# Attention steps placed directly behind the query projection, and another order of the first expert loads

## The reference

```python
u, v, q = proj[..., :256], proj[..., 256:768], proj[..., 768:]
y_pool = pool_mixer(u, w_pool, pool_scale)            # window means 2/4/8/16 minus the token, a linear map
a, gate = split(v); glu = a * sigmoid(gate)
y = depthwise_conv(glu, 31 taps) + b_dw
y_conv = silu(layer_norm(y, conv_norm_g, conv_norm_b))   # mean and variance over 256 channels, per token
y_mem = softmax(q @ k^T / sqrt(128)) @ v_mem          # 4 heads, 256 memory tokens, k and v from mem_n @ w_kv
x = layer_norm(alpha * x + concat(y_pool, y_conv, y_mem) @ w_out)
scores = sigmoid(x @ w_router); top 8 of 64 experts per token
x = layer_norm(alpha * x + routed experts + 1 shared expert)   # each (silu(x@wg) * (x@wu)) @ wd, width 256
```

## Time and profile before

| | |
|---|---|
| median of 3 runs | 1431.15 us (1430.84 to 1432.0) |
| the profiled execution | 1432.97 us, of which 1431.4 us is the span from its first to its last instruction |
| TensorE busy / VectorE busy | 1319.7 us (92%) / 966.2 us (68%) |
| mean granted TensorE clock | 0.959 of full speed |

### The profile page before, as it was taken

How to read it: one execution, slowest core, us unless ns; L and a number is a source line. 1 busy time by engine, 2 the same in 40 slices (tenths; PEclk the granted TensorE clock), 3 DMA queues, 4 the chain that set the end, 5 groups by cost and what they waited for, 6 DMA issues and landing times.

```text
span 1431.4 us, 25695 instructions
## 1 busy us (share of the span) xinstructions
PE 1319.7 (92%) x6367; PEld 1087.3 (76%) x6368; DVE 966.2 (68%) x1120; ACT 799.1 (56%) x1057; POOL 467.3 (33%) x430
## 2 busy tenths in 40 slices
PE   8967936799999699999999999999999999999974
PEld 6865725578887588888888888888888888888851
DVE  4889657467766387757579555556677579777737
ACT  4121256412225396857579566556767578777724
POOL 0000020136655243333344333333333344333322
PEclk9989978799999899999999999999999999999988
DMA  6112041122334999888799978788899899999755
GB/s 238 45 53 80 0 175 40 59 84 80 89 110 157 363 320 329 306 308 278 237 329 372 312 219 257 240 252 301 251 310 316 273 327 347 331 329 322 210 178 228
DMA packets 77969, 324.11 MB, mean 226 GB/s; under 512 B 22560, under 2 KB 24768, under 8 KB 52720
## 3 DMA queue, kind: packets, MB, share of 16 engines
q1 hardware_dynamic: 43056, 251.05, 47.1%
q0 software_dynamic: 33728, 68.47, 20.5%
q10 hardware_dynamic: 1152, 4.19, 0.7%
HBM read 290.51 MB, written 67.72 MB: 250 GB/s over the span
## 4 chain that ended last, share of the span: by engine, by line
PE 80%; DVE 11%; DMA 3%; issue 2%; ACT 1%; POOL 1%; SPq 0%; POOLq 0%; ACTq 0%; DVEq 0%
PE ps L1650 37%; PE ps L1668 18%; PE ps L1443 7%; PE ps L1557 6%; PE ps L1468 4%; DVE cv L1030 4%; PE ps L1593 2%; PE ps L1681 1%; PE ps L1582 1%; PE ps L1544 1%; DVE whl L944 1%; DMA sum_d<-ysb,idx 1%; POOL list_d L548 1%; DVE pr L1125 1%; DMA xin<-in_x 1%
## 5 line engine op out<-in xcount | busy, mean ns | idle before, releaser
L1650 PE MATMUL ps<-wgu,xTe 128*128 x2304 | 550.3, 394 | 2.2 <-issue 2.0
L1650 PEld LDWEIGHTS ps<-wgu,xTe 128*128 128x128 f32 x2304 | 426.8, 188 | 89.9 <-issue 4.4
L601 POOL DMA_INDIRECT sum_d<-ysb,idx x95 | 176.2, 1854 | 510.6 <-ACT ysb L829 439.5
L1668 PE MATMUL ps<-wdn,hT 128*128 (+1 forms) x1236 | 299.4, 391 | 0.0
L1311 DVE TENSOR_TENSOR wgu<-raw,wgu (+1 forms) x128 | 287.7, 2289 | 8.4 <-issue 3.5
L1668 PEld LDWEIGHTS ps<-wdn,hT 128*128 128x128 f32 x1236 | 232.7, 189 | 48.4
L757 ACT CAST wgu<-raw (+1 forms) x128 | 246.9, 1930 | 1.6 <-SPq L424 1.6
L1316 DVE TENSOR_TENSOR xTe<-ps,xTe 128x512 fp32r<-128x512 f32 x194 | 124.6, 685 | 141.3 <-ACT xTe L824 141.3
L829 ACT ACTIVATE ysb<-ps,idx 128x512 f32<-128x512 f32 x188 | 119.3, 686 | 122.5 <-PE ps L1668 122.5
L1311 DVE TENSOR_TENSOR wdn<-raw,wdn x64 | 146.7, 2293 | 59.5 <-ACT wdn L817 59.1
L591 POOL DMA_INDIRECT xg<-x_d,idx x99 | 110.2, 1113 | 49.5 <-issue 27.5
(11 more groups left out here) (226 smaller groups left out, 1152.6 us busy)
## 6 DMA issues: line engine op xcount, KB each, us to landing
raw<-in_w_gate SPq DMA_DIRECT2D x64, 1024.0 KB, 11.4
raw<-in_w_up SPq DMA_DIRECT2D x64, 1024.0 KB, 8.6
raw<-in_w_down SPq DMA_DIRECT2D x64, 1024.0 KB, 9.3
wraw<-in_w_in SPq DMA_DIRECT2D x10, 512.0 KB, 3.4
xin<-in_x SPq DMA_DIRECT2D x8, 512.0 KB, 7.3
wraw<-in_w_kv SPq DMA_DIRECT2D x8, 512.0 KB, 3.2
raw<-in_w_out SPq DMA_DIRECT2D x4, 1024.0 KB, 8.1
xres<-in_x SPq DMA_DIRECT2D x8, 512.0 KB, 5.1
```

What stands on the lines that cost most here:

```text
L601: g.indirect_dma_start(out=sums, out_offset=bass.IndirectOffsetOnAxis(ap=idx[:, c % RING, c % 2:c % 2 + 1], axis=0), in_=ysb[:, c % 2], in ...
L1650: last = mm(ps[:, 2 + s, :], xTe[:, s, st, d], wgu[:, w, mo, d].rearrange("p a n -> p (a n)"), start=(d == 0 and st == 0 and mo == 0), sto ...
L1668: last = mm(ps[:, down_bank(i) + h, :], hT[:, s, st, c], wdn[:, w, mo, c, h * 512:(h + 1) * 512].rearrange("p a n -> p (a n)"), start=(c = ...
```

## The change

In the projections: `memT` is split in u0; u0 and u1 have 8 taps each, q1 4, q2 9 and q3 13; the pooling parts stand in q0 (three) and q1 (two), and `pool0`, `pool1` behind q1. The jobs `mean` and `var` are gone from `JOBS`, as is the meeting of the engines at `s_endP`. The LayerNorm of the convolution is done within the tiles of the attention: mean behind the first two `scores`, its subtraction ahead of tile 0, squares in tile 0, the sum of squares in tile 1 as 16 products with one column each (a variance per token along partitions), its power -0.5 on GpSimd for 8 elements per partition, a diagonal matrix of it on DVE in tile 2 (`spread`), its product with the matrix of 1/256 on PE in tile 3 (constants 2^-16 and -0.5 make up for the 1/256), the scaling on DVE and Silu on ACT in tile 3. PE waits for the scaling before the transposes of tile 3. `w_out` lands in a buffer of its own (`wor`) and is split in tiles 4 to 7.

In the experts: SP loads expert 2 one matrix after the other without waiting for the list, and expert 3 only when the first two gathers have landed. GpSimd reads the number of items and the first three list addresses before it waits for the last scatters.

```diff
@@ jobs @@
-        JOBS = W_JOBS[:15] + ["pool0", "pool1"] + W_JOBS[15:17] + ["mean", "q3", "var"]
+        JOBS = W_JOBS[:16] + ["pool0", "pool1"] + W_JOBS[16:18]
-        TAPS_IN = {"gate1": 8, "a1": 4, "u0": 10, "u1": 10, "q0": 8, "q1": 8, "q2": 6}
+        TAPS_IN = {"gate1": 8, "a1": 4, "u0": 8, "u1": 8, "q1": 4, "q2": 9, "q3": 13}
-            POOL_IN = ["K2", "K3", "V0", "V1", "V2"]
+            POOL_IN = {"q0": (0, 1, 2), "q1": (3, 4)}
@@ SP @@
-                sp.dma_start(raw[:, 2 + n], a["w_out"][n]).then_inc(s_wo[n], 16)
-            sp.wait_ge(s_endP, 4)
+                sp.dma_start(wor[:, 2 * n:2 * n + 2].rearrange("p c n -> p (c n)"), a["w_out"][n]).then_inc(s_wo[n], 16)
+            sp.wait_ge(s_mix, 2)
...
                 load(e, 0, slot_of(e0, 0))
+                if e0 == 2:
+                    landed(e0, 0, rounds)
...
                 load(e, 1, slot_of(e0, 1))
+                if e0 == 2:
+                    landed(e0, 1, rounds)
...
-            sp.wait_ge(s_idx[0], 16)
             load_expert(2, 0)
+            for s in range(2):
+                sp.wait_ge(s_xg[s], 16)
             load_expert(3, 0)
@@ GpSimd @@
-            g.sem_inc(s_endP, 1)
-            g.wait_ge(s_endP, 4)
+            g.wait_ge(s_norm_v, 1)
+            g.tensor_tensor(rv[:, 1], rv[:, 0], half8[:], ALU.pow).then_inc(s_rstd, 1)
+            g.wait_ge(s_mix, 2)
...
+            g.wait_ge(s_tabs, 1)
+            n_items = g.value_load(nit[0:1, 0:1], min_val=NT + E, max_val=MAX_ITEMS)
+            firsts = [g.value_load(tab[0:1, 2, RING + j:RING + j + 1], min_val=0, max_val=LIST - 128)
+                      for j in range(3)]
             for s in range(2):
                 g.wait_ge(s_sc[s], 16 * K * 4)
-            g.wait_ge(s_tabs, 1)
-            n_items = g.value_load(nit[0:1, 0:1], min_val=NT + E, max_val=MAX_ITEMS)
...
             for j in range(3):
-                load_pairs(1, j)
+                g.dma_start(idx[:, j], list_d[bass.ds(firsts[j], 128), :]).then_inc(s_idx[j], 16)
@@ ScalarE, in the attention loop @@
+                if t == 0:
+                    centred_squares()
...
+                if t == 3:
+                    conv_out()
+                if t >= 4:
+                    wo_hi(t - 4)
@@ VectorE @@
+            def centre():
+                v.wait_ge(s_norm_pe, 1)
+                for c in range(2):
+                    step(V.tensor_tensor(cv[:, c], cv[:, c], ps[:, 6:8, :].rearrange("p a n -> p (a n)"), ALU.subtract))
+            def variance():
+                v.wait_ge(s_norm_pe, 2)
+                V.tensor_scalar(rv[:, 0], ps[:, 6, 0:NT], EPS, 2.0 ** -16, ALU.add, ALU.mult).then_inc(s_norm_v, 1)
+            def spread_rstd():
+                v.wait_ge(s_rstd, 1)
+                V.tensor_tensor(spread[:], ident[:].unsqueeze(1).to_broadcast([128, NT, 128]),
+                                rv[:, 1].unsqueeze(2).to_broadcast([128, NT, 128]), ALU.mult).then_inc(s_norm_v, 1)
+            def scale():
+                v.wait_ge(s_norm_pe, 3)
+                for c in range(2):
+                    step(V.tensor_tensor(cv[:, c], cv[:, c], ps[:, 6:8, :].rearrange("p a n -> p (a n)"), ALU.mult))
...
+            centre()
             probabilities(0)
             for t in range(NT):
+                if t == 1:
+                    variance()
+                if t == 3:
+                    scale()
...
+                if t == 2:
+                    spread_rstd()
...
+                if t >= 4:
+                    wo_lo(t - 4)
@@ TensorE @@
+            def conv_variance():
+                pe.wait_ge(s_sq, 1)
+                for t in range(NT):
+                    for c in range(2):
+                        last = mm(ps[:, 6, t:t + 1], buf1[:, c, t * 128:(t + 1) * 128], ones[:, 0:1],
+                                  start=(c == 0), stop=(c == 1))
+            def conv_rows():
+                pe.wait_ge(s_norm_v, 2)
+                for h in range(2):
+                    last = mm(ps[:, 6 + h, :], ones[:], spread[:, 4 * h:4 * h + 4].rearrange("p a n -> p (a n)"),
+                              start=True, stop=True)
...
             scores(0)
             scores(1)
+            conv_mean()
+            pe.wait_ge(s_gfree[0], len(JOBS) // 2)
             for t in range(NT):
                 if t + 2 < NT:
                     scores(t + 2)
+                if t == 1:
+                    conv_variance()
+                if t == 3:
+                    conv_rows()
+                    pe.wait_ge(s_yn, 1)
```

More of the change, by code:

```diff
@@ L109, in build @@
         wrt = at("wrt", 176, [128, 2, ND, E], R)
-        pr = at("pr", 184, [128, 2, HEADS, M])
+        pr = at("pr", 193, [128, 2, HEADS, M])
+        rv = at("rv", 207.125, [128, 2, NT])
+        spread = at("spread", 185, [128, NT, 128])
         oh = at("oh", 194, [128, K, E])
@@ L164, in build @@
         mv = at("mv", 206.90625, [128, 2, 2])
-        sm = at("sm", 192, [128, 2, 3, HEADS])
+        sm = at("sm", 201.75, [128, 2, 3, HEADS])
+        half8 = at("half8", 201.84375, [128, NT])
         tokf = at("tokf", 207.03125, [128, 2])
@@ L212, in build @@
         s_cvd = sem("s_cvd")
+        s_norm_pe = sem("s_norm_pe")
         s_yc = sem("s_yc")
         s_sq = sem("s_sq")
-        s_sd = sem("s_sd")
+        s_norm_v = sem("s_norm_v")
+        s_rstd = sem("s_rstd")
         s_yn = sem("s_yn")
@@ L498, in _ @@
             g.memset(epst[:], EPS).then_inc(s_pool, 1)
-            g.wait_ge(s_pool, 5)
+            g.memset(half8[:], -0.5).then_inc(s_pool, 1)
+            g.wait_ge(s_pool, 6)
             g.affine_select(out=ident[:], in_=ident[:], compare_op=ALU.not_equal, fill=1.0, base=0,
@@ L668, in _ @@
                     nc.scalar.copy(memT[:, 0, 4:8], mtmp[:, 4:8]).then_inc(s_mhi, 1)
-                if w != "mean" and w != "var":
-                    act.wait_ge(s_job, j + 1)
+                act.wait_ge(s_job, j + 1)
                 if w[:4] == "gate":
@@ L690, in _, with centred_squares, conv_out, wo_hi @@
                     nc.scalar.activation(mixA[:, c], both, ACT.Copy, scale=cpar[:, 3, c:c + 1]).then_inc(s_gfree[s], 1)
[L691 to L709, removed]
+            def centred_squares():
+                act.wait_ge(s_yc, 1)
+                nc.scalar.activation(buf1[:, :, 0:S], cv[:], ACT.Square).then_inc(s_sq, 1)
+            def conv_out():
+                act.wait_ge(s_yn, 1)
+                for c in range(2):
+                    nc.scalar.activation(mixA[:, 2 + c], cv[:, c], ACT.Silu, bias=cpar[:, 2, c:c + 1],
+                                         scale=cpar[:, 1, c:c + 1]).then_inc(s_mix, 1)
+            def wo_hi(n):
+                act.wait_ge(s_wo[n], 16)
+                nc.scalar.copy(wo[:, 0, 2 * n:2 * n + 2], wor[:, 2 * n:2 * n + 2]).then_inc(s_wohi, 1)
+            act.wait_ge(s_diff, 1)
+            for n in range(2):
+                act.wait_ge(s_gfree[n], len(JOBS) // 2)
             def q_hi(t):
@@ L1043, in _ @@
                     v.sem_inc(s_mtc, 1)
[L1044 removed]
+                if w == "u0":
                     for b_ in range(2):
@@ L1067, in _ @@
                                         ALU.subtract).then_inc(s_gfree[1], 1)
[L1068 to L1088, removed]
-            assert tap == len(taps)
-            for n in range(4):
+                for part in POOL_IN.get(w, ()):
+                    pooling(part)
+            assert tap == len(taps)
+            settle()
+            v.sem_inc(s_cvd, 1)
+            def centre():
+                v.wait_ge(s_norm_pe, 1)
+                for c in range(2):
+                    step(V.tensor_tensor(cv[:, c], cv[:, c], ps[:, 6:8, :].rearrange("p a n -> p (a n)"), ALU.subtract))
+                settle()
+                v.sem_inc(s_yc, 1)
@@ new lines, in variance @@
+            def variance():
[9 more added lines that the diff above has]
+                    step(V.tensor_tensor(cv[:, c], cv[:, c], ps[:, 6:8, :].rearrange("p a n -> p (a n)"), ALU.mult))
+                settle()
+                v.sem_inc(s_yn, 1)
@@ L1488, in _ @@
                         last = mm(ps[:, b + h, :], bd[:, c], diff[:, c, h * 512:(h + 1) * 512], start=True, stop=True)
-                elif w in ("mean", "var"):
-                    pe.wait_ge(s_const, 8)
-                    pe.wait_ge(s_cvd if w == "mean" else s_sq, 1)
-                    src = cv if w == "mean" else buf1
-                    for h in range(2):
-                        for c in range(2):
-                            last = mm(ps[:, b + h, :], ones[:], src[:, c, h * 512:(h + 1) * 512],
-                                      start=(c == 0), stop=(c == 1))
                 last.then_inc(s_job, 1)
@@ L1501, in _, with conv_mean @@
                         transpose_tile(memin[:, m], 2 * m).then_inc(s_mt, 1)
-            pe.wait_ge(s_job, len(JOBS))
-            pe.sem_inc(s_endP, 1)
-            pe.wait_ge(s_endP, 4)
+            def conv_mean():
+                pe.wait_ge(s_gfree[1], len(JOBS) // 2)
```

(19 more changed lines are left out.)

12 lines of the change are left out of this document (5 added, 7 removed).

## The result

| | before | changed |
|---|---|---|
| median | 1431.58 us (1430.84 to 1433.16, 4 runs) | 1412.08 us (1408.09 to 1413.79, 4 runs) |
| span of the profiled execution | 1431.4 us | 1411.8 us |

The ratio is 0.9853, interval [0.9834, 0.9872]: 19.5 us faster. The forecast was 1403 us, the range 1396 to 1413. The sign and the range held; the number is 9 us too low.

What follows compares the result with a forecast made beforehand. TensorE, busy 92% of the span, was taken as the bound, so only its waits counted: −22 up to the first projection and −6.2 at the first gathers, −28.2 on 1432.97, gave 1404.8, so 1403 us beside the median; range 1396 to 1413.

Steps and rivals of the forecast that it cites:

- the projections: Projections up to the last tap: it ends at about 172 us and the attention starts there instead of 206.92, −35.
- the attention: From the queries' split to the first output projection: 13 us added to 65.9, so that projection starts at 251 instead of 272.86.
- The variance products: In the attention's tile 1: 16 products of one column each, taken as 4.2 us, bounded by 1 and 14.
- the term of −6.2: At the turn to the experts: the first gather lands 5.3 us earlier, and 0.9 us comes from the clock.
- 0 to 2.5 us are added, and I take 1.2: Ahead of the first gathers: expert 2's loads in flight make the last scatters land 1.2 us later.
- three issues: Between the wait for scatters and the gather: three issues at 0.9 us remain, so the gather is issued 2.4 us earlier.
- The term's 0.9 us for the clock: PE's first pieces behind the first gather: a shorter idle may hold the clock, saving 0.9 of 3.3 us.
- My first rival: At the turn to the experts: the first gathers bring nothing, only 0 to 2.4 us are left, 1407 to 1409; chance 0.17.
- its second way: At the last scatters ahead of the first gathers: they land late by as much as the gather would gain.
- its first: At the first gathers: a gather takes its 9 us by itself, even without loads beside it.
- nothing lost behind it: Behind the first gathers, in the expert loop: PE waits nowhere, so the whole −28.2 us reaches the end.
- my rival of a loop bound by transfers: Expert loop of 97 items: 0.29 us per item would undo the gain, at 0.35 us 1437; chance 0.03.

Runs made afterwards that it cites:

- The old order: The changed kernel with taps, `memT` and pooling in the order of the kernel before, LayerNorm still inside the attention: 0.9871 of the kernel before.
- the loads held: The changed kernel with expert 2's three loads also waiting until both first gathers have landed: 0.9805 of the kernel before, 1406.43 us.
- the experts' part alone: The kernel before with only the new order of the first expert loads and of GpSimd's register reads: 0.9982 of the kernel before, 1430.63 us.

## Why the prediction was right in sign and 9 us off

**Right: the projections.** K0's wait is gone, K1's is 4.48 us (4.5 forecast), the last tap ends at 173.4 (172). DVE's wait for the last weight is 5.95 (5.7). The old order shows that the new one is needed for the early split of the queries: without it q3 is late (how much of that reaches the end stays open, as said above).

**Right in this profile: the attention.** From the queries' split to the first projection it takes 77.9 us (251.42 − 173.53), 12.0 more than before (13 forecast), and the first projection stands at 251.4 (251 forecast). The variance products, the one cost without a row, took 4.06 us (4.2). That was in part luck. In six other profiles with the same work ahead of it, the first projection stands between 251.4 and 254.5, and the four at 253.8 or later all have the variance products at 6.82 us, as the changed kernel's first repeat has:

```profile
190.00 6.82 PE L1536 MATMUL ps<-ones,buf 128*128 128x1 f32 x32
```

The granted clock was 0.50 there from 190.5 to 196.5 us, and 0.88 in the first profile from 189.5 to 193.4. The forecast took these products from transposes at the higher level and had no term for the lower.

Silu starts 1.30 us after the start of its table load, and the load starts where the cast ahead of it ends (208.40 + 0.59), so no drain shows. The Trainium skill (page "ScalarE: Activation LUTs", section "What ACT_TABLE_LOAD costs") puts a switch at about 2.66 us with its drain; this case's trace disagrees with it.

**Wrong: the first gathers, the term of −6.2.** Of its parts, the gather's own time was right (4.54 us, 3 to 5 forecast). The step that failed is "0 to 2.5 us are added, and I take 1.2" for what expert 2's loads do to the last scatters, together with the list pieces, which were given three issues and no price for a load in flight. In the changed kernel GpSimd came through the wait for the scatters 3.8 us later than before, counted from the first projection (191.9 against 188.1; 191.4 and 191.7 in the repeats). The list piece took 3.5 us (4.5 and 4.0 in the repeats, 2.0 to 2.2 with no load in flight). The first ate 2.6 us more than the forecast had, the second about 2; the gather itself was 0.5 us shorter than the sum had it. The term's 0.9 us for the clock didn't come either: the first product took 7.09 us, against 7.15 before; with the loads held it took 6.25. The writes of the shared expert's results were slowed as well (ACT waits of 5.2, 4.0 and 3.8 us for them in the three profiles of the changed kernel), which stood nowhere in the sum, but PE waits for the gather behind them anyway.

With no load in flight the stage is 6.2, 6.0 and 5.3 us shorter than before in the three profiles where the gather is waited for and the reads stand ahead. That the first of these equals the forecast's sum is chance: the forecast had loads in flight, 5.3 us up to this point and 0.9 behind it. My first rival, that the gathers bring nothing, is what happened, by its second way (late scatters and what follows them), not by its first: a gather does take half the time when it has the DMA engines to itself. The rival's own time, 1407 to 1409, was too low by what was lost elsewhere.

The Trainium skill, page "DMA: Bandwidth & Descriptors", section "Queues, rings and completion order", has the DMA engines take turns between queues packet by packet. I drew from this that a gather never waits for SP's backlog. The rows don't contradict the rule but do contradict what I drew from it: taking turns with 4 MB doubled the gather (8.93 and 9.24 against 4.4 to 5.5 us), and taking turns with 1 MB doubled a list piece of 1.5 KB.

**Wrong: nothing lost behind it.** The sum let the whole shift reach the end. In the changed kernel's profile the shift is 22.8 us at the first item and 19.8 at the last. Most of it goes in one place, where experts of one item each follow one another and the DMA engines are 0.98 busy from 1214 to 1234 us (timeline of the changed kernel; SP hands the weights over late, and PE's next products take 7.35 us instead of 5.71, with a mean grant of 0.91 over the same stretch):

```profile
1214.37 1.91 ACT L773 CAST wgu<-raw  x1 [3.56 <-SPq L430]
...
1218.74 7.35 PE L1697 MATMUL ps<-wgu,xTe 128*128 x24 [1.25 <-ACT wgu L773]
```

This is my rival of a loop bound by transfers, over three items instead of 97. Eleven of the twelve further profiles have such a wait, of about 1 us; the fastest of them and the kernel before have none. What a profile loses in the whole loop ranges from nothing to some 5 us (5.1 with the experts' part alone); repeats of the changed kernel lost 1.3 and nothing. So its size changes from run to run, and what sets it stays open.

5 us at the turn and 3 in the loop are the 9 between 1403 and 1412, within a microsecond, but only in this profile. In the profiles of the two repeats the sum is much the same and the parts are others: the first projection comes 19.1 and 18.7 us earlier than before instead of 22, the turn brings 1.3 and 0.6 us, and the loop costs 1.3 and nothing. What repeats in all three is the miss at the turn.

## What to carry to other kernels

A transfer held back "until the gather has landed" must also be out of the way of what the gather itself waits for: scatters, address lists, result writes. Count every small transfer ahead of the one that is to be sped up and give each the price of a load in flight; holding the loads back cost nothing here: ACT waits up to 1.28 us for expert 2's weights, and PE never does. And where a vector engine's queue sets the pace, look at which job its last input stands behind: moving two products, 3.6 us together, by one place brought the attention forward by 5.5 us, nearly what the whole experts' edit was meant to bring.

## What the runs showed of the hardware that I had not expected

- A list piece of 1.5 KB took 1.97 to 2.17 us from issue to landing with no load in flight and 3.5 to 4.5 us with one load of 1 MB beside it (chains of waits of three and of four profiles).
- A gather of 512 KB took 4.4 to 5.5 us without large loads and 8.9 to 9.2 us with 4 MB issued about it.
- 32 fp32 passes with a single column each took 3.63 us at a granted clock of 0.99 and 6.82 us at 0.50, 0.11 and 0.21 us a pass. A transpose of 128 columns takes 0.13 and 0.25 us (1.03 and 1.97 for 8), so 127 columns less saved little.
- On one chip all four profiled kernels took 200.8 to 204.4 us from the first projection to the end of the shared expert, against 193.6 to 198.2 elsewhere, with ACT waits of 6.2 to 6.9 us that no row explains.
